# A second queue for half of the expert weights: ScalarE issues the odd blocks

## What is computed

```python
def moe_swiglu(h, router_w, w_in, w_out):
    logits = jnp.einsum('btd,de->bte', h, router_w)
    top_vals, top_idx = lax.top_k(logits, 2)
    gates = jax.nn.softmax(top_vals, axis=-1)
    combine = sum over the two choices of one_hot(top_idx, 8) * gates
    out = 0
    for e in range(8):
        g, u = split(h @ w_in[e])              # w_in[e]: 1024 x 7168
        out += combine[:, e] * ((silu(g) * u) @ w_out[e])    # w_out[e]: 3584 x 1024
    return out
```

## Time and profile before

| what | us |
|---|---|
| median of 3 runs | 1974.8 |
| lowest, highest | 1969.48, 1976.64 |
| the profiled execution: its time | 1977.56 |
| its span, first to last instruction | 1975.8 |
| TensorE busy in the span | 1820.3 |
| ScalarE busy in the span | 386.9 |

### The profile page before, as it was taken

The page is one execution under the profiler, slowest core; times in us unless marked ns, Lnnn a source line. Parts: engine busy times, 40 slices in busy tenths (PEclk is TensorE's granted clock), DMA queues, the critical chain, the costliest instruction groups (busy, mean ns, idle before and its releaser), DMA issues. The chain is left out here.

```text
span 1975.8 us, 35831 instructions
## 1 busy us (share of the span) xinstructions
PE 1820.3 (92%) x16214; PEld 1069.0 (54%) x16214; DVE 475.0 (24%) x762; ACT 386.9 (20%) x662; POOL 34.8 (2%) x71
## 2 busy tenths in 40 slices
PE   5999789999999889865799999999999999999995
PEld 2743478888888768544535345353443534435342
DVE  3313445222233663454310100101001010010103
ACT  3223433222232432342100000100001000010001
POOL 1000100000000000000000000000000000000000
PEclk8998899999999999987699999999999999999997
DMA  9255462332324232347599999999999999999970
GB/s 372 96 171 171 144 187 72 99 100 93 107 86 138 69 109 84 129 150 271 228 339 367 369 363 375 327 364 373 368 361 335 364 371 361 368 334 365 369 294 24
DMA packets 141160, 477.43 MB, mean 242 GB/s; under 512 B 11168, under 2 KB 35096, under 8 KB 122576
## 3 DMA queue, kind: packets, MB, share of 16 engines
q1 hardware_dynamic: 137344, 467.64, 64.5%
q0 software_dynamic: 3664, 7.48, 1.2%
HBM read 473.96 MB, written 1.13 MB: 240 GB/s over the span
## 5 line engine op out<-in xcount | busy, mean ns | idle before, releaser
L950 PE MATMUL ps<-w_hi,h_t 128*128 128x512 f32 (+1 forms) x960 | 298.2, 391 | 18.9 <-DVE h_t L1532 7.2
L950 PE MATMUL ps<-w_moe,h_te 128*32 128x256 f32 (+1 forms) x3520 | 296.6, 493 | 16.4 <-DVE residual L1876 16.4
L950 PE MATMUL ps<-h_t,w_hi 128*128 128x512 f32 (+1 forms) x768 | 222.5, 374 | 5.0 <-DVE h_t L1532 5.0
L950 PEld LDWEIGHTS ps<-w_moe,h_te 128*32 128x32 f32 x3520 | 113.2, 111 | 193.3 <-issue 138.9
L950 PE MATMUL ps<-w_raw,h_te 128*32 128x256 f32 (+2 forms) x3648 | 216.8, 396 | 0.0
L1479 DVE TENSOR_TENSOR w_lo<-w_raw,w_hi 128x2048 fp32r<-128x2048 f32 x58 | 132.9, 2292 | 349.0 <-ACT w_hi L619 348.5
L950 PEld LDWEIGHTS ps<-w_hi,h_t 128*128 128x128 f32 x960 | 182.6, 193 | 59.7 <-issue 8.3
L950 PE MATMUL ps<-w_lo,h_t 128*128 128x512 f32 (+1 forms) x480 | 186.9, 389 | 0.0
L1875 DVE TENSOR_TENSOR residual<-silu_g,ps 128x512 f32<-128x512 f32 (+1 forms) x32 | 19.8, 618 | 650.7 <-ACT silu_g L894 650.7
L619 ACT ACTIVATE w_hi<-w_raw 128x2048 fp32r<-128x2048 f32 x58 | 110.8, 1914 | 327.9 <-PE ps L950 319.4
L950 PEld LDWEIGHTS ps<-w_raw,h_te 128*32 128x32 f32 x3648 | 112.2, 110 | 100.9 <-issue 61.5
(11 more groups left out here) (233 smaller groups left out, 1213.6 us busy)
## 6 DMA issues: line engine op xcount, KB each, us to landing
w_moe<-in_expert_in_w_dram SPq DMA_DIRECT2D x110, 1024.0 KB, 6.2
w_raw<-in_expert_out_w_dram SPq DMA_DIRECT2D x62, 1024.0 KB, 7.1
w_raw<-in_expert_in_w_dram SPq DMA_DIRECT2D x50, 1024.0 KB, 7.7
w_raw<-in_ada_w_dram SPq DMA_DIRECT2D x48, 1024.0 KB, 5.0
w_moe<-in_expert_out_w_dram SPq DMA_DIRECT2D x34, 1024.0 KB, 7.0
work<-in_expert_in_w_dram SPq DMA_DIRECT2D x32, 1024.0 KB, 7.2
w_raw<-in_expert_in_w_dram SPq DMA_DIRECT2D x64, 512.0 KB, 4.8
w_raw<-in_ffn_in_w_dram SPq DMA_DIRECT2D x44, 512.0 KB, 4.9
```

Source lines behind the costliest of these rows:

```text
L950: return pe.matmul(out_, l, r, start=first, stop=last, skip_group_check=True)
```

## The change

In the first round SP fetches the even blocks only (its loops step by 2). The odd blocks from 15 on are fetched from ScalarE's queue, in unrolled code: behind each block's place in ScalarE's cycle a call `free(n)` waits until block n is used and issues the fetch of block n + 14, if that is odd. The first 14 blocks stay with SP, and so do the later rounds. To place the calls, ScalarE's cycle is rewritten as a loop over the blocks; each of its operations hangs on a certain block and stands ahead of that block's `free`. At the start of the stage eight calls of `free` stand between `hte` and the first `silu`. `fetch` is moved out, unchanged but for the queue as its parameter.

```diff
+    def fetch(queue, e, n):
+        kind, s_, b, ahead = ROUND[n]
+        w, done = moe_view(n), w_landed[n % RING]
...
         def refill(rnd, e, n, turns=0):
 
             sp.wait_ge(used, moe_base(rnd) + turns * EB + (n - RING + 1))
-            fetch(e, n)
+            fetch(sp, e, n)
...
+            step = 1 if rnd else 2
             with sp.Fori(0, NE - 2) as e:
-                for n in range(RING, EB + 8):
+                for n in range(RING, EB + 8, step):
                     refill(rnd, e, n, e)
-                for n in range(8, RING):
+                for n in range(8, RING, step):
                     refill(rnd, e + 1, EB + n, e)
-            for n in range(RING + EB * (NE - 2), len(ROUND)):
+            for n in range(RING + EB * (NE - 2), len(ROUND), step):
                 refill(rnd, (n - 8) // EB, n)
...
             def cycle(e, last=False):
-                transposed(e, 0)
-                silu(e, 1)
-                transposed(e, 1)
-                act.wait_ge(ptt_ready, NE * rnd + e + 1)
-                act.activation(PTR[0:CAP, :], ps[0:CAP, 7, 0:2 * P], ACT.Copy).then_inc(pt_done, 1)
-                silu(e, 2)
-                transposed(e, 2)
-                silu(e, 3)
-                if not last:
-                    hte(NE * rnd + e + 2)
-                transposed(e, 3)
-                if not last:
-                    silu(e + 1, 0)
-                yhi(e, last)
+                at = len(ROUND) - len(LAST) if last else 8
+                for n in range(at, len(ROUND) if last else 8 + EB):
+                    kind, s_, b, ahead = ROUND[n]
+                    if (kind, s_, b) == ("in", 1, 1):
+                        transposed(e, 0)
+                    if kind == "in" and b == WIDTH[s_] // P - 1:
+                        silu(e + 1 if ahead else e, s_)
+                    if (kind, s_, b) == ("in", STEPS - 1, 3) and not last:
+                        hte(NE * rnd + e + 2)
+                    if kind == "out" and s_ < STEPS - 1 and b == 1:
+                        transposed(e, s_ + 1)
+                    if (kind, s_, b) == ("out", 0, 3):
+                        act.wait_ge(ptt_ready, NE * rnd + e + 1)
+                        act.activation(PTR[0:CAP, :], ps[0:CAP, 7, 0:2 * P], ACT.Copy).then_inc(pt_done, 1)
+                    if (kind, s_, b) == ("out", STEPS - 1, 1):
+                        yhi(e, last)
+                    if not rnd:
+                        free(n if last else n + e * EB)
+
+            def free(n):
+
+                m = n + RING
+                if m % 2 and m < len(ROUND):
+                    act.wait_ge(used, base + n + 1)
+                    fetch(act, (m - 8) // EB, m)
 
             hte(NE * rnd + 1)
+            if not rnd:
+                for n in range(8):
+                    free(n)
             silu(0, 0)
```

More of the change, by code:

```diff
@@ L434, in moe_view @@
         return ring(n).rearrange("p (k u n) -> p k u n", k=2, u=2)
+    def fetch(queue, e, n):
+        kind, s_, b, ahead = ROUND[n]
+        w, done = moe_view(n), w_landed[n % RING]
+        e = e + ahead if ahead else e
+        if kind == "out" and s_ < STEPS - 1:
+            rows = expert_out_w[0, e, 1024 * s_ + 256 * b:1024 * s_ + 256 * b + 256, :]
+            queue.dma_start(w, rows.rearrange("(p j) n -> p j n", j=2)).then_inc(done, 16)
+        elif kind == "out":
+            rows = expert_out_w[0, e, 1024 * s_ + 256 * b:1024 * s_ + 256 * b + 256, :]
+            queue.dma_start(w, rows.rearrange("(j p) n -> p j n", p=P)).then_inc(done, 16)
+        elif s_ < STEPS - 1:
+            rows = expert_in_w[0, e, b * P:(b + 1) * P, :].rearrange("p (u n) -> p u n", u=2)
+            queue.dma_start(w, rows[:, :, 1024 * s_:1024 * s_ + 1024]).then_inc(done, 16)
+        else:
+            for u in range(2):
+                rows = expert_in_w[0, e, 2 * b * P:(2 * b + 2) * P, ED * u + 1024 * s_:ED * u + ED]
+                queue.dma_start(w[:, :, u, :], rows.rearrange("(k p) n -> p k n", p=P)).then_inc(done, 16)
     Z_BANK = (6, 3)
@@ L506, in experts @@
                         sp.wait_ge(used, B_MOE)
-                    fetch(0, n)
+                    fetch(sp, 0, n)
             else:
```

## The result

| kernel | median of 20 runs, us | lowest, highest |
|---|---|---|
| before | 1974.65 | 1969.31, 1980.96 |
| changed | 1978.45 | 1971.39, 1982.14 |

The ratio is 1.0022, with an interval of 1.0012 to 1.0032: the change costs 3.8 us by the medians, between 2.4 and 6.3 us by the interval, and is within 0.5% of the kernel before. A single run of either could stand on either side; only many runs tell them apart.

The account below looks back on a forecast made before the run. TensorE was taken to bound the kernel, with transfers covered by the lead. The start's 1.8 us plus the clock's 1.7 us gave +3.5 us on 1974.8, so 1978.3 us, range 1970 to 1988.

Parts of the forecast that it names:

- The bound: First-round expert stage: TensorE sets the pace and waits for no transfer; 361 GB/s is what it asks for.
- What leaves SP: 161 odd-block refills leave the SP queue, whose time isn't on the path: 0 us.
- 161 issues on ScalarE, 80.5 us, cost 0: Refill issues over the expert stage, 0.333 to 0.543 us each or 32 x 0.373, hidden in ScalarE's idle time.
- The start: First silu of the stage: block 21's issue (0.54) and the table load (1.28) enter the chain restarting TensorE, +1.8 us.
- The drain ahead of the load: At the first silu's table load, the skill's drain of about 1.38 us would make the start cost 3.2 us.
- The clock behind the start: Two blocks after the lengthened first stall run at the lower clock, 7.06 instead of 5.37 us: +1.7 us.
- The clock behind the seven: Seven later 2.0 us stalls at cycle heads, three followed by slow blocks; a changed count could give -5.1 to +6.8 us.
- The copies behind the silu: At a cycle's head, one 0.33 us issue precedes the six expert-output copies, hidden by 9.4 us of slack: 0.
- The transfers, cost 0: Expert stage: two queues feed the same 16 engines the same bytes; landings fit the 38 us lead, no gain possible.
- The rival of two queues that move less: Engines switching between two streams fall under 361 GB/s in the expert stage: +10 to +60 us, chance 0.07.
- The same sum for the profiled execution: Whole kernel: the +3.5 us put on the profiled execution's 1977.56 us, giving 1981.1 us.

Follow-up runs that it names:

- The price without cover: Changed kernel with the next expert's first silu put behind the cycle's last refill, so an issue precedes each recurring handoff; 1.0024 on the kernel before.
- the experiment with the late load: Kernel before with a tiny ScalarE copy, waiting for the eighth block, ahead of the first silu, so the table loads after that wait; 1.0004.
- the short lead: First-round refills held back to go out 3 blocks before need instead of 13: kernel before 1.0022, changed kernel 1.0148, changed with every refill on time 1.0131.
- the exact wait: Next expert's first silu waits only for the last block it reads, two blocks earlier: kernel before 1951.92 us, changed kernel 1955.53 us.

## Why the prediction was right

Forecast 1978.3 us, measured 1978.45, within 0.5% of the kernel before, as forecast.

- **The bound.** Right. TensorE paces the stage, its wait list names no transfer before or after, and when it was sped up by 21 us the transfers followed at 365 GB/s.
- **What leaves SP.** Right: 0. SP waited 689 us in 312 pieces and now waits 799 us in 156: it has more time to spare, not less.
- **161 issues on ScalarE, 80.5 us, cost 0.** Right in place and size: 0.547 and 0.334 us each; the pairs are longer, 0.438, and the eight blocks of the last output step, taken at 0.543 at most, take 0.385. All 322 refills on ScalarE cost no more than half of them. The price without cover, 7 x 0.5 = 4 us, was measured too: 4.6 us of longer stalls, 0.65 us each, since the handover comes on top of the issue.
- **The start.** Right, and with the clock behind it the loss that the stage shows: 1.8 us expected on the stall, 1.94 found (0.66 for the issue with its handover, 1.28 for the load). The load did land behind the refill; it starts at 988.78 and not behind 991.7, as this execution came to the stage 2.25 us earlier and had 1.3 us less in its first blocks. Moving one call took the loss away.
- **The drain ahead of the load.** The trace decides against the larger sum by the Trainium skill (ScalarE: Activation LUTs, What ACT_TABLE_LOAD costs) for this place: the load starts 0.08 us behind the issue (988.14 + 0.56 = 988.70, 988.78), the silu 0.02 us behind the load. With ScalarE idle ahead of it the switch costs the 1.28 us of the load alone. In the experiment with the late load it is the same right behind a small copy: the copy ends at 986.35, the load starts at 986.36.
- **The clock behind the start.** Right: 7.06 us. All six stalls of 3.5 to 4.0 us at the first silu, one in each of six traces, were followed by 6.9 to 7.1 us.
- **The clock behind the seven.** The count stayed at three of seven, so neither -5.1 nor +6.8 came. It was three in the changed kernel's second trace too, and two or three in each of the others with 2.0 us stalls and the full lead. The total came out because the same number of them was met, which the prediction had said it couldn't tell.
- **The copies behind the silu.** Expected 0.33 us later, hidden by 9.4 us of slack. They are not later at all, see the last section.
- **The transfers, cost 0.** Right for this kernel, but one step of the argument was too wide: the row said that landings of 9.4 us fit a lead of 38, and the text made of it that two queues cost nothing. They do cost, in the longest landings; the lead covers it. The rival of two queues that move less named a loss of rate as its mechanism; what the short lead shows is later landings, and its threshold is the lead, not the rate: at the full lead and with the exact wait two queues moved 366 GB/s, one 365. The rule that the prediction takes from the Trainium skill (DMA: Bandwidth & Descriptors, Issuing engines are not separate DMA queues), that several issuing engines save only issue time, fits the full lead, where two queues bring nothing; with the short one they cost 25 us beyond one queue, and the runs decide.

That forecast and median agree within 0.2 us is partly luck: the measured cost is known to 2.4 to 6.3 us only, and the steps were each right to some tenths of a us. The same sum for the profiled execution, 1981.1, came out 3.1 us too high (1978.03): what this execution lost in the stage, 2.7 us, it had nearly gained ahead of it by starting the stage 2.25 us earlier.

## What to carry to other kernels

Ask first whether any engine waits for the transfers. Here none did, and a second queue had nothing to give; the 2 us stall in the same chain of waits, from a wait set two blocks too late, was worth 21 us. Where refills are put among an engine's own operations, look at what they displace: the one refill ahead of a first silu pushed a table load into the path, and each refill inherits the waits of what stands ahead of it. A large lead hides late refills and longer landings, though not the table load, so try the change with a short lead before calling it free.

## What the runs showed of the hardware

- **An issue from ScalarE runs beside its operations, but only those ahead of it.** Timeline of the changed kernel behind a cycle's end:

```profile
1235.85 0.60 ACT L894 ACTIVATE silu_g<-ps 128x512 f32<-128x512 f32 x1 [30.64 <-PE ps L965]
1235.86 0.33 ACTq L443 DMA_DIRECT2D w_raw<-in_expert_out_w_dram  x1
1236.35 0.38 ACT L895 ACTIVATE silu_g<-ps 128x256 f32<-128x256 f32 x1
1236.61 1.20 ACT L909 ACTIVATE y_split<-ps 96x512 fp32r<-96x512 f32 x2
...
1237.23 0.55 ACTq L449 DMA_DIRECT2D w_raw<-in_expert_in_w_dram  x1
...
1237.82 1.53 ACT L909 ACTIVATE y_split<-ps 32x256 fp32r<-32x256 f32 x4
```

The issue at 1235.86 runs under the silu that started at 1235.85, and the one at 1237.23 under the copies. From the silu's start to the end of the copies it is 3.50 us (1237.82 + 1.53 less 1235.85), as before (1606.03 + 2.74 less the start of that silu):

```profile
1605.27 0.60 ACT L893 ACTIVATE silu_g<-ps 128x512 f32<-128x512 f32 x1 [30.64 <-PE ps L950]
```

An operation behind an issue that had to wait does pay it: 0.66 us.
- **Two hardware queues in turn lengthen the longest landings.** At the full lead and the same rate (357 to 366 GB/s) the longest landing of a 1 MB input block was 10.1 to 12.5 us in the seven traces with two queues and 9.0 to 9.8 in the four with one. It isn't ScalarE's queue as such: with every refill on ScalarE the line reads

```profile
DMA to landing us min/median/max: 5.1/7.4/9.8
```

For the pairs it is 9.7 to 10.8 us with two queues against 6.6 to 7.9. At the short lead the pairs take 10.5 to 11.1 us at most against 8.4, there at 347 to 348 GB/s against 357.
- **A pause of about 2 us is followed by the lower clock in some cases only:** 19 of the 49 recurring stalls of 2.0 us in seven traces with the full lead. There it was never two in a row, but with the short lead it was (one queue, the stalls that end at 1240.15 and 1363.88 us). It costs 1.7 us over two blocks.
